# Kernel study: first transfers in another order, the first norm moved between the adaptive sums, rotation tables computed later, and token scaling on ScalarE before the first two turns

## The reference

```python
cos, sin = rope_tables(positions)
cond = jax.nn.silu(c)
for i in range(DEPTH):                     # DEPTH = 2
    shift, scale, gate = jnp.split(cond @ ada_w[i] + ada_b[i], 3, axis=-1)
    h = rms_norm(x, norm_g[i]) * (1 + scale[:, None, :]) + shift[:, None, :]
    ...
    y = nsa_mixer(h, cos, sin, ...) if i % 2 == 0 else moba_mixer(h, cos, sin, ...)
    x = x + gate[:, None, :] * y
```

## Time and profile before

| | us |
|---|---|
| median of three runs | 969.85 (969.57 to 970.19) |
| the profiled execution's own time | 970.32 |
| its span | 968.5 |
| TensorE busy | 905.7 (94%) |
| VectorE busy | 573.8 (59%) |
| ScalarE busy | 484.2 (50%) |

### The profile page before, as it was taken

One profiled execution on the slowest core, in us unless ns is written; L12 is line 12 of the kernel. 1 busy time (PEld: TensorE's weight loads), 2 busy tenths in 40 slices (PEclk: granted clock), 3 DMA queues, 4 the chain that ended last, 5 costly groups with the idle time before them and its releaser, 6 DMA issues.

```text
span 968.5 us, 13044 instructions
## 1 busy us (share of the span) xinstructions
PE 905.7 (94%) x5021; PEld 778.5 (80%) x5021; DVE 573.8 (59%) x917; ACT 484.2 (50%) x756; POOL 175.6 (18%) x192
## 2 busy tenths in 40 slices
PE   2779898999889999999999999999999899999998
PEld 2568897899778988888888888888789788888886
DVE  4884577444866637755555446767356665555543
ACT  2143574455544645654545447586663555444431
POOL 1006335255206441000000001452001100000000
PEclk9889998999989999999999999999999999999999
DMA  9855646155646255555555565553234556555650
GB/s 344 312 162 179 204 143 232 44 153 149 197 135 198 78 161 180 165 183 187 178 195 195 175 178 185 162 154 110 68 107 143 163 180 199 185 175 180 210 175 22
DMA packets 45693, 163.26 MB, mean 169 GB/s; under 512 B 5185, under 2 KB 5441, under 8 KB 45633
## 3 DMA queue, kind: packets, MB, share of 16 engines
q1 hardware_dynamic: 45632, 162.44, 52.6%
HBM read 161.37 MB, written 1.05 MB: 168 GB/s over the span
## 4 chain that ended last, share of the span: by engine, by line
PE 85%; DVE 8%; ACT 3%; issue 1%; DMA 1%; POOL 1%; SPq 0%; DVEq 0%; ACTq 0%
PE bank L481 56%; PE bank L490 11%; PE bank L505 4%; DVE w_lo L1517 2%; PE bank L645 2%; PE bank L534 1%; DVE mx L1670 1%; PE bank L651 1%; DVE ada_acc L1617 1%; DMA w_raw<-in_weights 1%; PE bank L728 1%; PE bank L671 1%; PE bank L673 1%; PE bank L672 1%; ACT kh L1038 1%
## 5 line engine op out<-in xcount | busy, mean ns | idle before, releaser
L1034 ACT ACTIVATE w_hi<-w_raw 128x1024 fp32r<-128x1024 f32 (+2 forms) x249 | 258.9, 1046 | 194.4 <-PE bank L481 161.0
L1517 DVE TENSOR_TENSOR w_lo<-w_raw,w_hi 128x1024 fp32r<-128x1024 f32 (+2 forms) x249 | 304.6, 1241 | 81.9 <-ACT w_hi L1034 81.3
L481 PE MATMUL bank<-w_hi,h_hi 128*128 128x512 f32 (+1 forms) x576 | 229.3, 398 | 16.3 <-DVE w_lo L1517 8.2
L481 PE MATMUL bank<-w_hi,h_lo 128*128 128x512 f32 (+1 forms) x576 | 225.6, 392 | 0.0
L481 PE MATMUL bank<-w_lo,h_hi 128*128 128x512 f32 (+1 forms) x576 | 225.1, 391 | 0.0
L481 PEld LDWEIGHTS bank<-w_hi,h_hi 128*128 128x128 f32 x576 | 109.5, 190 | 38.9 <-issue 17.9
L481 PEld LDWEIGHTS bank<-w_hi,h_lo 128*128 128x128 f32 x576 | 109.2, 190 | 22.9
L481 PEld LDWEIGHTS bank<-w_lo,h_hi 128*128 128x128 f32 x576 | 109.4, 190 | 21.1
L2277 POOL TENSOR_TENSOR ada_acc<-ada_acc,w_raw 128x512 f32<-128x512 f32 x56 | 78.2, 1396 | 101.6 <-ACT w_raw L1038 96.3
L490 PE MATMUL bank<-h_hi,w_hi 128*128 128x256 f32 x264 | 79.6, 302 | 3.7 <-DVE tokq L1599 3.0
L490 PE MATMUL bank<-h_hi,w_lo 128*128 128x256 f32 x264 | 77.1, 292 | 0.0
(11 more groups left out here) (297 smaller groups left out, 1351.0 us busy)
## 6 DMA issues: line engine op xcount, KB each, us to landing
w_raw<-in_weights SPq DMA_DIRECT2D x298, 512.0 KB, 3.8
w_raw<-in_weights SPq DMA_DIRECT2D x4, 360.0 KB, 4.4
x<-in_x SPq DMA_DIRECT2D x1, 1024.0 KB, 6.5
gate_row<-in_gate_bias SPq DMA_DIRECT2D x2, 512.0 KB, 10.1
out<-x SPq DMA_DIRECT2D x4, 256.0 KB, 3.2
w_raw<-in_weights SPq DMA_DIRECT2D x3, 256.0 KB, 2.7
const<-in_constants SPq DMA_DIRECT2D x1, 413.5 KB, 7.1
cols<-in_columns SPq DMA_DIRECT2D x1, 208.5 KB, 2.5
```

Source lines behind the costliest of these rows:

```text
L481: mm = e.matmul(pb[t][:, 0:n], xs[q], ws[p], start=(k + kk == 0 and i == 0), stop=(k + kk == kts - 1 and i == 2))
L1034: e.activation(w_hi[i % NSPLIT][:, 0:c], raw[v % NRAW][:, 0:c], ACT.Copy).then_inc(*rounded(v))
L1517: e.tensor_tensor(w_lo[i % NSPLIT][:, 0:c], raw[v % NRAW][:, 0:c], w_hi[i % NSPLIT][:, 0:c].bitcast(F32), ALU.subtract).then_inc(*rested(v))
```

## The change

Four things are altered. SP issues the second weight unit before x and the third before the constants, and the positions, the row vectors and the gate bias go behind all units ahead of `nsa_q0`. VectorE runs `mac_chunk(2, 0)` before the first norm's means, does not wait for the power any more, takes the rest of `nsa_kcvc`[2] ahead of the second pair of ada columns, and computes the rotation angles and tables among the units of `nsa_q0`. ScalarE scales the tokens of the first two norms into `scr` (`norm_scales`), and TensorE turns `scr` by a transpose against the identity (`turn`) where it multiplied x by the diagonal. ScalarE's two sines move along.

```diff
@@ norm_turns (TensorE)
                     for t in range(TT):
-                        w.wait_ge(*diag_done.at((i, t)))
-                    if kp < 3 or i == 0:
-                        w.wait_ge(*free[kp])
-                    else:
-                        w.wait_ge(*(modulated.at((i, 0)) if i < 2 else h_rested.at((i, 1))))
-                    for kk in range(2):
-                        for t in range(TT):
-                            o = kk * S + t * P
-                            mm = e.matmul(b[:, o:o + P], x[:, t, (2 * kp + kk) * P:(2 * kp + kk + 1) * P],
-                                          diag[:, t, :], start=True, stop=True)
-                    mm.then_inc(*x_turned((i, kp)))
+                        w.wait_ge(*x_scaled.at((i, kp // 2, t)))
+                    w.wait_ge(*(free[kp] if kp < 3 or i == 0 else modulated.at((i, 0))))
+                    turn(b, [(kk * S + t * P, scr[:, t, (2 * kp + kk) * P:(2 * kp + kk + 1) * P])
+                             for kk in range(2) for t in range(TT)]).then_inc(*x_turned((i, kp)))
@@ ScalarE
+            def norm_scales(i, *after):
+
+                w.wait_ge(*norm_power.at(i))
+                for at in after:
+                    w.wait_ge(*at)
+                for j in range(2):
+                    for t in range(TT):
+                        half = slice(j * 512, (j + 1) * 512)
+                        copy(scr[:, t, half], x[:, t, half], scale=norm_rs[i][:, t:t + 1]).then_inc(*x_scaled((i, j, t)))
...
                     square_half(0, t, j, x_in.at())
+            norm_scales(0)
             w.wait_ge(*const_in.at())
...
+            rounds(of["nsa_kcvc"][2], 0)
             norm_rounds(0, (2, 3))
             rounds(of["nsa_kcvc"][2])
-            w.wait_ge(*turns_reduced.at())
-            e.activation(sin_t[:, :], ang[:, :], ACT.Sin).then_inc(*sin_done())
-            w.wait_ge(*cos_reduced.at())
-            e.activation(cos_t[:, :], cos_t[:, :], ACT.Sin).then_inc(*cos_done())
...
+            norm_scales(1, c_turned.at(1))
             norm_rounds(1)
@@ VectorE
             mac_chunk(0)
-            norm_factors(0)
-            mac_chunk(2)
+            mac_chunk(2, 0)
+            norm_means(0)
+            mac_chunk(2, 1, 2, 3)
+            rests(of["nsa_kcvc"][0], 0)
             ada_column(0, banks[0])
-            rests(of["nsa_kcvc"][0], 0)
             ada_column(2, banks[2])
...
             mac_chunk(3, 2, 3)
+            rests(of["nsa_kcvc"][2], 0)
             ada_column(1, banks[4])
             ada_column(3, banks[5])
             norm_modulates(0, (2, 3))
-            rotation_angles()
-            rests(of["nsa_kcvc"][2])
-            rotation_tables()
             rests(of["nsa_kcvc"][2])
...
                 if j == 0:
+                    rotation_angles()
                     head_sums("nsa_kskw")
+                if j == 1:
+                    rotation_tables()
                 if j == 2:
                     head_scales("nsa_kskw")
...
-            norm_factors(1)
+            norm_means(1)
             norm_modulates(1)
@@ SP
             fetch(0)
+            fetch(1)
             e.dma_start(x[:, :, :], x_d.rearrange("o (t p) d -> p (o t) d", p=P)).then_inc(*x_in())
+            fetch(2)
             e.dma_start(const[:, :], const_d).then_inc(*const_in())
-            fetch(1)
+            for u in range(3, of["nsa_q0"][0]):
+                fetch(u)
             e.dma_start(pos[:, :], pos_d).then_inc(*pos_in())
             e.dma_start(rows[:, :], rows_d.to_broadcast([P, NROWS])).then_inc(*rows_in())
-            for u in range(2, NRAW):
-                fetch(u)
             e.dma_start(gate_row[:, :], gate_bias_d[0:1, :].to_broadcast([P, D])).then_inc(*bias0_in())
-            for u in range(NRAW, of["moba_z0"][0]):
+            for u in range(of["nsa_q0"][0], of["moba_z0"][0]):
                 fetch(u)
```

More of the change, by code:

```diff
@@ L322, in program @@
                                 "gate_row_done"))
+        x_scaled = signal("x_scaled")
         squared, norm_mean, norm_power, diag_done, x_turned, modulated, h_rounded, h_rested = (
@@ L1219, in scalar @@
             head_squares("nsa_kskw", squared.at((0, 1, 1)))
-            for u in of["nsa_q0"]:
+            for j, u in enumerate(of["nsa_q0"]):
                 rounds(u)
+                if j == 0:
+                    w.wait_ge(*turns_reduced.at())
+                    e.activation(sin_t[:, :], ang[:, :], ACT.Sin).then_inc(*sin_done())
+                    w.wait_ge(*cos_reduced.at())
+                    e.activation(cos_t[:, :], cos_t[:, :], ACT.Sin).then_inc(*cos_done())
             head_squares("nsa_q0", hn_summed.at(("nsa_kskw", 1)))
@@ L1536, in norm_factors @@
                 w.wait_ge(*norm_power.at(i))
-                if i:
-                    w.wait_ge(*x_turned.at((0 if i == 1 else 1, 3)))
                 for t in range(TT):
```

## The result

The changed kernel takes **962.86 us** in the median (962.05 to 963.58, 4 runs), the kernel before 970.02 beside it (969.57 to 970.63, 4 runs): ratio 0.9926, interval 0.9914 to 0.9939. A second series gave 962.29 (960.78 to 965.8, 6 runs) against 969.95, ratio 0.9927 (0.9907 to 0.9946). One of the 24 executions of the kernel before beside the first four experiments took 2313.85 us and is left out of their ratios. The profiled execution took 962.59 us, 7.7 less than that of before.

A forecast was written before the change was run, and what follows sets the result against it. TensorE, busy for 94% of the span, was taken to bound the kernel by its work and waits. Gains of 1.9 + 4.8 + 0 + 0 = 6.7 us off 970.32 gave 963.6, or 963.1 for the median; range 960.3 to 965.8.

The forecast's parts named there:

- Part 1, the start: From 0 to 27.48 us: earlier transfers and the norm's transposes let modulation begin 1.9 us earlier (0.5 to 2.6).
- Part 2, the pause: TensorE's gap from 47.14 to 55.15 us: with `w_lo` ahead of the columns, TensorE starts 4.8 us earlier.
- Clock behind the pause: Behind the gap at 47.14 us: the clock falls despite about 3.2 us idle, so the warm-up is paid as today.
- rival that the clock stays up: At 48 us, warm-up not paid, 1.5 to 2 us more; chance 0.22, shared with the start gaining all 2.6: 961 to 962.
- Part 3, rotation: Angles and tables among the units of `nsa_q0`: `head_scales` comes later but within the slack before `compress_up`; cost 0.
- rival that the tables and the power exclude each other: VectorE's tables and GpSimd's power run one behind the other, TensorE waits 1.9 us: gain 4.8, median 965.0; chance 0.06.
- Part 4, norm 1: Norm 1's turns by transposes: first product 1.2 us earlier, set against a lower clock; 0 taken, from -0.7 to +0.4.
- transposes' rival: Transposes leave the clock down: the start gives 0.7 or nothing, norm 1 takes 0.7; median 965.1; chance 0.2.

The follow-up runs named there:

- first four experiments: Four follow-up runs measured together beside the kernel before, which took 970.43 us there.
- after_again: The whole change once more, unchanged, on the same chip: 962.29 us.
- rot_only: The kernel before with only `w_lo` of `nsa_kcvc`[2] ahead of the columns and the rotation moved: 966.13 us, ratio 0.9945.
- no_norm: The whole change without its norm parts, both norms turned by the diagonal as before: 962.8 us, ratio 0.9915.
- fill48: The whole change with ten products whose result nothing uses, in the pause ahead of `nsa_kcvc`[2]: 959.2 us, ratio 0.9889.
- fillT48: The whole change with 24 transposes of the identity in the pause ahead of `nsa_kcvc`[2]: 960.7 us, ratio 0.9902.
- fill4: The whole change with unused products ahead of `nsa_kcvc`[2], `nsa_gate` and norm 1's turns, and 24 transposes before the first turns: 955.12 us, ratio 0.9851.
- norm_only: The kernel before with only the norm parts and their order of columns and `w_lo`; transfers and rotation as before: 969.91 us, ratio 0.9993.
- diag1: The whole change with norm 1 turned by the diagonal again, norm 0 still by scaled tokens: 964.1 us, ratio 0.9939.

## Why the prediction was right, and where its terms were off

The forecast of 963.1 us and its way were right: transfers free the start, `w_lo` ahead of the columns and the angles out of the way shorten the pause, rotation and norm 1 hardly matter. That the sum came out to 0.3 us is luck: the start gave 1.4 more than forecast in the profiled execution, and the clock behind the pause and VectorE's stretch took 1.4 back. Point by point:

**Part 1, the start: 1.9 forecast, 3.3 in the profiled execution, 2.3 in the second (25.22).** The transfers came out as worked out, each step 0.3 to 0.9 us earlier. Of the 1.4 us over the forecast some 0.8 are the earlier start of the turns (18.41 for 19.2): the power ended at 16.94, for the transfers came 0.3 earlier and the two units ahead of the means took 2.6 us and not 3.2 (the first instruction of a chunk takes 0.48 us, the others 0.76). The turns took 3.64 us for 3.5. The other 0.6 are the columns, mis-sized as up to twice as long at the lower clock (24.5 to 26.4): they ended at 23.77, and in `after_again`, where they did take 3.41 us, at 24.79. The range stopped at 2.6 although its own fastest case (sums at 21.8, columns 1.84, 0.6 to the modulation) gives 3.2. The gain was also credited to the wrong part: the transfers alone give 2.7, and the shorter turns nothing, because the later power and the scaling ahead of them cost what they save.

**Part 2, the pause: 4.8 forecast, 4.5 measured.** From first modulation to `nsa_kcvc`[2] it is 23.15 us (24.19 to 47.34) for 27.67. The missing 0.3 is VectorE's stretch between the two modulations, taken as fixed: 20.50 us for 20.09, with an idle time of 0.53 at 41.62. The chain has 0.47 of it as "issue", time in which VectorE waited for nothing that the profile shows. All nine profiles in which norm 0 has its new parts show 0.52 or 0.53 there, none of the five with the diagonal at norm 0 does. So it came with the norm parts; why stays open. The `w_lo` ahead of the columns cost nothing: from the last sum to the modulation it is 1.5 us before and now. `rot_only` confirms the term alone: 4.8 earlier (50.31).

**Clock behind the pause: "paid as today" was 1.1 too kind** in the profiled execution (10.8 us for three units, 9.65 before) and 0.2 in `no_norm` (46.93 to 56.82, 9.9). My rival that the clock stays up fell. Its price, 1.5 to 2 us below what is paid before, was about right: `fill48` takes 8.3 us for 9.65, 1.4 less, and 2.5 less than the whole change.

**Part 3, rotation: 0 forecast, 0 measured.** No idle time of VectorE ahead of `head_scales`, no wait ahead of `compress_up`. The rival that the tables and the power exclude each other fell: the power took 2.96 us beside the tables. GpSimd's two steps in the kernel before, whose groups above don't have them:

```profile
72.74 0.26 POOL L2249 TENSOR_SCALAR stats<-stats 128x16 f32<-128x16 f32 x1 [54.65 <-DVE stats L1579]
73.09 3.84 POOL L2252 TENSOR_TENSOR stats<-stats 128x16 f32<-128x16 f32 x1
```

Together they last 4.19 us there and 4.20 now (68.47 to 72.67).

**Part 4, norm 1: 0 forecast (-0.7 to +0.4), 0.6 at equal clock, 1.0 with the clock low for longer.** Over the range. The first product was mis-sized: 4.9 us behind the power's end (265.77 to 270.63), where the forecast had 5.8 and the kernel before 7.0. Read from the two first profiles alone it would have been 1.9.

**The transposes' rival fell in its mechanism.** The rule of the Trainium skill (TensorE: Matmul & The Clock Gate, Part 4: PE-mode transpose), that transposes don't count as busy, isn't what `fillT48` and `fill4` show for these float32 transposes. Its consequence, cold columns, did occur in three of the eight profiles with sixteen transposes, and in none of the five with the diagonal's 5.4 to 6.4 us. Why in some and not in others stays open; no run moved the start of the turns alone. That the norm parts as a whole give nothing measurable fits these rows: nothing at the start, 0.4 us lost at 41 us, 0.6 to 1.0 gained at norm 1.

**Sum.** At `compress_up` the gain is 3.3 + 4.5 - 1.1 = 6.7 us. The profiled executions end 7.7 apart. On the way the distance is 5.6 (160.90 to 155.30), 7.05 (251.56 to 244.51), 4.2 (255.41 to 251.19, behind a low stretch that only the changed kernel has), 6.2 (286.65 to 280.49) and 7.5 (753.46 to 745.94). So the last 1.0 can't be given to the change. The medians differ by 7.2 and 7.7, the parts' own medians add up to 2.2 + 4.3 + 0.5 = 7.0, of which the 0.5 (`norm_only`) isn't clear of noise.

## What to carry to other kernels

Order the first transfers by what is needed first, and put an instruction that the next product needs ahead of a wait that it can fill: alone they gave 2.2 and 4.3 us in the median, of 2.7 and 4.8 at their place in the profile. Work out a pause's price with the clock behind it: filling three pauses and warming up ahead of the first work with useless products gave as much again (962.3 to 955.1) as the whole change. A difference of two profiled executions over one stage is only evidence when their low-clock stretches are of equal length there; compare several profiles by that length.

## What the runs showed of the hardware that I had not expected

- Transposes of 128x128 in fp32 hold the clock up (24 of them, 2.84 us) and bring it up from the start: 24 in 4.61 us as TensorE's first work, then eight in 1.06 us (0.13 each), where sixteen with no work ahead of them took 3.65 (0.22 each).
- The granted clock shows 1.00 ahead of the first fall even where TensorE runs at the lower level: `after_again` has no row below 1.00 from 20 to 28 us, while its columns take 3.41 us for 1.84. Its products behind them, at 28.54 and read as 1.00 too, take 0.63 us each, as those of the first profile do where it reads 0.50. There only durations tell. One such stretch of `after_again`:

```profile
23.00:24.00 1.00, 1.00 (x6) 1.00 (x6) 0.16 (x1) 0.00 (x0) 0.00 (x0) 1.00 1.03 410
```

- A 3.1 us pause costs 1.3 to 2.7 us in the three units behind it (9.6 to 11.0 us for 8.3). The clock fell at that pause in each of the five profiles that had it, for 3.4 us in `no_norm` and `diag1` and for 6.8 in the whole change, `after_again` and `rot_only`.
- GpSimd's step on 128x16, 0.26 us before, took 1.16 beside a `w_lo` (68.30 to 69.51), and ended 0.1 us behind it. By itself that isn't a loss, since both steps together last as long as before. In both first profiles a GpSimd product for the rotation of 128x32 shows it more clearly: 1.24 us beside a `w_lo` (89.26 before, 82.58 after), and 0.25 in the same instruction 1.2 us earlier. That agrees with the Trainium skill (SBUF — State Buffer, Who interferes with whom) for a VectorE instruction of 1.2 us with two inputs; beside the tables of 0.17 us no such delay shows.
